# Gate and up projections by pairs of tiles: four of sixteen k blocks as two 2x2 block products of seven, and both tiles transposed together

## What is computed

```python
def _swiglu(x, w_gate, w_up, w_down):
    return (jax.nn.silu(x @ w_gate) * (x @ w_up)) @ w_down

x = _layer_norm(DEEPNORM_ALPHA * x + m, ln1_g, ln1_b)
x = _layer_norm(DEEPNORM_ALPHA * x + _swiglu(x, w_gate, w_up, w_down), ln2_g, ln2_b)
```

## Time and profile before

| | us |
|---|---|
| median of 3 runs | 943.72 (943.58 to 944.22) |
| the profiled execution, its own time | 944.1 |
| its span (first to last instruction) | 942.3 |
| PE busy in the span | 936.5 |
| DVE busy | 707.5 |
| ACT busy | 470.6 |
| POOL busy | 85.3 |

### The profile page before, as it was taken

The page is one execution under the profiler, slowest core; times in us unless marked ns, Lnnn a source line. Parts: engine busy times, 40 slices in busy tenths (PEclk is TensorE's granted clock), DMA queues, the critical chain, the costliest instruction groups (busy, mean ns, idle before and its releaser), DMA issues.

```text
span 942.3 us, 12166 instructions
## 1 busy us (share of the span) xinstructions
PE 936.5 (99%) x4466; PEld 786.0 (83%) x4466; DVE 707.5 (75%) x1146; ACT 470.6 (50%) x644; POOL 85.3 (9%) x78
## 2 busy tenths in 40 slices
PE   9999999999999999999999999999999999999997
PEld 8999988888888888888888888888888888888885
DVE  6778566588687776777777776776779987799777
ACT  5686764463444444444444444444445654465550
POOL 0105530000022020202020300000000000000000
PEclk9999999999999999999999999999999999999999
DMA  9844224593555655555555555555547666356632
GB/s 362 321 149 167 103 90 179 186 362 128 217 196 206 209 193 184 204 191 183 206 190 178 178 193 209 203 195 183 205 152 288 253 236 243 134 195 236 237 135 90
DMA packets 28102, 187.81 MB, mean 199 GB/s; under 512 B 3104, under 2 KB 3616, under 8 KB 6560
## 3 DMA queue, kind: packets, MB, share of 16 engines
q1 hardware_dynamic: 28032, 187.31, 54.5%
q0 software_dynamic: 32, 0.00, 0.0%
HBM read 183.11 MB, written 4.19 MB: 199 GB/s over the span
## 4 chain that ended last, share of the span: by engine, by line
PE 99%; DVE 0%; ACT 0%; DVEq 0%; issue 0%; ACTq 0%
PE acc L1535 58%; PE acc L1732 20%; PE acc L1473 5%; PE tp L1732 4%; PE acc L1394 4%; PE acc L1672 2%; PE acc L1507 1%; PE tp L1586 1%; PE tp L1521 1%; PE tp L1599 1%; PE tp L1383 0%; PE tp L1612 0%; PE tp L1611 0%; PE tp L1610 0%; PE tp L1628 0%; PE acc L1798 0%
## 5 line engine op out<-in xcount | busy, mean ns | idle before, releaser
L1535 PE MATMUL acc<-w_hi,act_t 128*128 128x512 f32 x1344 | 413.9, 389 | 0.0
L1038 DVE TENSOR_TENSOR w_lo<-raw,w_hi 128x1024 fp32r<-128x1024 f32 x191 | 236.3, 1251 | 124.8 <-ACT w_hi L753 123.9
L753 ACT ACTIVATE w_hi<-raw 128x1024 fp32r<-128x1024 f32 x184 | 194.8, 1061 | 246.3 <-PE acc L1535 244.3
L1535 PEld LDWEIGHTS acc<-w_hi,act_t 128*128 128x128 f32 x1344 | 252.4, 188 | 52.2
L1535 PE MATMUL acc<-w_lo,act_t 128*128 128x512 f32 x672 | 261.5, 389 | 0.0
L853 ACT ACTIVATE w_hi<-raw 128x512 fp32r<-128x512 f32 (+1 forms) x154 | 115.2, 782 | 100.1 <-PE acc L1732 85.9
L1732 PE MATMUL acc<-w_hi,hid_t 128*128 128x512 f32 x504 | 161.1, 389 | 0.0
L1217 DVE TENSOR_TENSOR w_lo<-raw,w_hi 128x512 fp32r<-128x512 f32 (+1 forms) x154 | 131.6, 880 | 35.9 <-ACT w_hi L853 35.6
L1535 PEld LDWEIGHTS acc<-w_lo,act_t 128*128 128x128 f32 x672 | 126.2, 188 | 26.3
L1732 PEld LDWEIGHTS acc<-w_hi,hid_t 128*128 128x128 f32 x504 | 94.6, 188 | 19.7
L1186 DVE STREAM_TRANSPOSE turned<-hid 32x128 f32<-32x128 f32 x352 | 106.6, 303 | 5.6
(11 more groups left out here) (214 smaller groups left out, 982.1 us busy)
## 6 DMA issues: line engine op xcount, KB each, us to landing
raw<-in_w_gu SPq DMA_DIRECT2D x88, 1024.0 KB, 4.8
raw<-in_w_down SPq DMA_DIRECT2D x44, 1024.0 KB, 5.0
raw<-in_w_out SPq DMA_DIRECT2D x16, 1024.0 KB, 4.8
raw<-in_x_w SPq DMA_DIRECT2D x14, 552.0 KB, 7.2
raw<-in_w_uq SPq DMA_DIRECT2D x4, 1024.0 KB, 7.7
raw<-in_w_ukv SPq DMA_DIRECT2D x4, 1024.0 KB, 6.0
ln_rows<-in_ln_rows SPq DMA_DIRECT2D x4, 1024.0 KB, 10.3
raw<-in_w_qidx SPq DMA_DIRECT2D x2, 1024.0 KB, 6.1
```

What stands on the lines that cost most here:

```text
L753: act.activation(w_hi[:, (2 * slot + half) % RING, 0:n], raw[:, slot, first:first + n], ACT.Copy).then_inc(hi_done, 1)
L1038: dve.tensor_tensor(w_lo[:, h, 0:n], raw[:, slot, first:first + n], w_hi[:, h, 0:n], ALU.subtract).then_inc(lo_done, 1)
L1535: last = pe.matmul(acc[:, bank0 + t, :], lhs[:, k, x, t * P:(t + 1) * P], part[:, w, n * GC:(n + 1) * GC], start=(start and x == 0 and par ...
```

## The change

Tiles 2 to 21 become ten pairs (p = 1 to 10; tile 2p is "first", 2p+1 is "second"). For four of the 16 k blocks the pair is one problem of two 2x2 blocks: (two halves of the tokens) x (two k blocks) times (two k blocks) x (two tiles), done twice for the two groups q of k blocks, and summed. The seven products are P1, P5, P6, P7, P2, P3, P4 in this order, each 2 groups x 3 = 6 matmuls. The left factors are blocks of the input or their sums `s_gate`, formed once by POOL. The right factors are blocks of the weights or their sums, which DVE forms in place in `raw` (`pair_sum`, four of 1024 columns for each pair). The other 12 k blocks are six plain steps for each tile. A step is still 1024 columns of `w_hi` and `w_lo`. The order of the steps is `FFN_STEPS`: the last three plain steps of the second tile of the pair before, seven products, six plain steps of the first tile, three of the second.

The products share banks. P1 goes to bank 1 of the second tile and stays there; P6 is added to it in place, then P7. After P1, after P6 and after P7 ACT copies that bank to another one (`seeded`): into the first tile's bank 0, negated into the second tile's bank 0, into the first tile's bank 1. There P2, P3 and P4 and the plain steps are added. P5 has a bank of its own, `tp[2]`; ACT copies it to `y_s` and DVE adds it to the second tile (`add_y`).

Transposes are done for both tiles of a pair at once: 16 instructions for a pair, each over 256 elements of a partition where it was 128, in four lots behind steps 2 to 5 of the next pair's first tile. `hid_hi` and `hid_lo` are one instruction for a pair. The first sum that POOL made is now made in place in `turned`, so `s_t` has three sums. Weights of a pair are loaded as 12 pieces of 512 KB and two of 1 MB; the first pair's two go to `quad_1`.

```diff
+def ffn_sequence():
+    steps = []
+    for p in range(1, PAIRS):
+        ends = [(p - 1, "second", n) for n in range(PLAIN - 3, PLAIN)] if p > 1 else [None] * 3
+        steps += ends + [(p, "product", n) for n in (P1, P5, P6, P7, P2, P3, P4)] + [(p, "first", 0)]
+        steps += [(p, "first", n) for n in range(1, PLAIN)] + [(p, "second", n) for n in range(PLAIN - 3)]
@@ SP
+            load_tile(0)
+            for q in range(2):
+                load_quad(1, q)
+            load_tile(1)
+            for n in range(PLAIN_SLOTS):
+                load_plain(1, n)
             sp.wait_ge(x1_done, TOK * CHUNKS)
             sp.dma_start(x1_rows, xn[:]).then_inc(x1_stored, 16)
@@ ACT
+            def hi_step(p, kind, n):
+                v = V_OF[p, kind, n]
+                if kind == "product":
+                    if n == P1:
+                        for q in range(2):
+                            act.wait_ge(quad_full[q], 16 * p)
+                    elif n in SUM_OF:
+                        act.wait_ge(pair_t_done, 4 * (p - 1) + SUM_OF[n] + 1)
+                    act.wait_ge(*used_step(v - RING))
+                    act.activation(by_quad(w_hi[:, v % RING, :]), quad(p, SOURCE[n]), ACT.Copy).then_inc(hi_done, 1)
...
+            def before_hi(v):
+                for p in range(1, PAIRS):
+                    first, second = banks_of(2 * p), banks_of(2 * p + 1)
+                    for n, dst, sign in ((P1, first[:, 0, :], 1.0), (P6, second[:, 0, :], -1.0),
+                                         (P7, first[:, 1, :], 1.0)):
+                        if v == V_OF[p, "product", n] + RING:
...
+                            act.wait_ge(*used_step(V_OF[p, "product", n]))
+                            act.activation(dst, second[:, 1, :], ACT.Copy, scale=sign).then_inc(seeded, 1)
...
+                if v - RING in FFN_ENDS:
+                    silu_step(2 + FFN_ENDS.index(v - RING))
@@ DVE
+            for p, kind, n in FFN_STEPS:
+                before_lo(V_OF[p, kind, n])
+                lo_step(p, kind, n)
+                if (kind, n) == ("product", P1):
+                    pair_sum(p, B11, B11, B12)
+                    pair_sum(p, B12, B12, B22)
+                if (kind, n) == ("product", P5):
+                    pair_sum(p, B11, B11, B22)
+                if (kind, n) == ("product", P2):
+                    pair_sum(p, B21, B11, B21)
+                if (kind, n) == ("first", 2):
+                    add_y(p)
+                if kind == "first" and n >= 2:
+                    turn_hid(p - 1, n - 2)
...
             for u in range(len(DOWN_UNITS)):
                 if u == 3:
-                    gate_up(TILES - 1, 1)
+                    gate_up(TILES - 1)
+                if u == 9:
+                    hid_lo(PAIRS - 1)
...
-                if u == 3:
-                    turn_hid(TILES - 1, (0, 1))
-                if u == 4:
-                    turn_hid(TILES - 1, (2, 3))
-                if u == 7:
-                    hid_lo(TILES - 1)
+                if 3 <= u < 7:
+                    turn_hid(PAIRS - 1, u - 3)
@@ PE
+            def pair_product(p, n):
+                first, second = banks_of(2 * p), banks_of(2 * p + 1)
+                out = {P1: second[:, 1, :], P5: tp[:, 2, :], P6: second[:, 1, :], P7: second[:, 1, :],
+                       P2: first[:, 0, :], P3: second[:, 0, :], P4: first[:, 1, :]}[n]
...
+                if n in (P6, P7, P4):
+                    pe.wait_ge(seeded, 3 * p - 2 + (P6, P7, P4).index(n))
+                pe.wait_ge(lo_done, v + 1)
+                for q in range(2):
+                    for x, part in ((0, w_hi), (0, w_lo), (1, w_hi)):
+                        last = pe.matmul(out, factor(q, Q_FACTOR[n], x), part[:, v % RING, q * GC:(q + 1) * GC],
...
```

More of the change, by code:

```diff
@@ L822, in ffn_tile @@
                     if h == 3:
-                        silu_step(i - 1, 1 - c)
+                        silu_step(0)
                     if h == 6:
[L825 to L837, removed]
+                        act.wait_ge(x1_stored, 16)
+                        act.wait_ge(g_step, 5)
+                        act.activation(s_gate[:, 0, :, :, :], g_sum[:], ACT.Copy).then_inc(g_hi, 1)
+            SOURCE = {P1: B11, P5: B11, P6: B11, P7: B12, P2: B21, P3: B22, P4: B21}
@@ L840, in down_hi_unit @@
+            tile_1()
+            for p, kind, n in FFN_STEPS:
+                before_hi(V_OF[p, kind, n])
+                hi_step(p, kind, n)
+                if (kind, n) == ("second", PLAIN - 4):
+                    hid_hi(p - 1)
+                if (kind, n) == ("product", P5) and 2 <= p < len(DOWN_QUADS) + 2:
+                    q = p - 2
+                    act.wait_ge(s_step, 4 * q + 4)
+                    act.activation(s_t[:, q, 0, :, :], s_sum[:], ACT.Copy).then_inc(s_hi, 1)
             def down_hi_unit(u):
@@ new lines, in pair_sum, with before_lo @@
+            def pair_sum(p, dst, x, y):
+                dve.tensor_tensor(quad(p, dst), quad(p, x), quad(p, y), ALU.add).then_inc(pair_t_done, 1)
+            def before_lo(v):
+                if v - RING in FFN_ENDS:
+                    gate_up(2 + FFN_ENDS.index(v - RING))
+                if v - RING == V_PAIRS - 1:
+                    gate_up(1)
+                for p in range(1, PAIRS):
+                    if v == V_OF[p, "second", PLAIN - 4] + 1:
+                        hid_lo(p - 1)
@@ new lines, in pair_plain @@
+            def pair_plain(p, tile, n):
+                out = banks_of(2 * p + (tile == "second"))
+                v, k0, end = V_OF[p, tile, n], PAIR_K + 2 * n, n == PLAIN - 1
+                if (tile, n) == ("first", 0):
+                    pe.wait_ge(seeded, 3 * p)
+                if (tile, n) == ("second", 0):
+                    pe.wait_ge(y_added, 2 * p)
+                pe.wait_ge(lo_done, v + 1)
+                for m in range(2):
+                    for t in range(TOK):
+                        for x, part in ((0, w_hi), (0, w_lo), (1, w_hi)):
+                            last = pe.matmul(out[:, t, :], act_t[:, k0 + m, x, t * P:(t + 1) * P],
+                                             part[:, v % RING, m * GC:(m + 1) * GC], start=False,
+                                             stop=(end and (m, x) == (1, 1)), skip_group_check=True)
+                last.then_inc(*((ffn_full, 1) if end else (pe_used, 1)))
@@ L1724, in _ @@
+            first_tile()
+            tile_1()
+            for p, kind, n in FFN_STEPS:
+                if kind == "product":
+                    pair_product(p, n)
+                else:
+                    pair_plain(p, kind, n)
             begun = {}
@@ L1828, in down_slot @@
         return down[list(tiles), :, :, pair, int(kind[1]) - 1].transpose(2, 0, 1, 3).reshape(P, -1)
+    gu = k_tiles(np.stack([gate, up], axis=2).reshape(D, 2 * FFN), 2 * FC)
+    later = gu[2:].reshape(PAIRS - 1, 2, P, KD, 2 * FC)
+    quads = later[:, :, :, 0:PAIR_K].reshape(PAIRS - 1, 2, P, 2, 2, 2 * FC).transpose(0, 2, 3, 1, 4, 5)
+    plain = later[:, :, :, PAIR_K:].transpose(0, 2, 1, 3, 4).reshape(PAIRS - 1, P, -1)
     arrays = {
```

325 lines of the change are left out of this document (231 added, 94 removed).

## The result

The median of the changed kernel is **952.21 us** (950.01 to 953.17, 4 runs), beside 943.97 us (943.58 to 944.51, 4 runs) for the kernel before: ratio 1.0084, interval 1.0069 to 1.0099. It is slower by 8.2 us; the forecast was 941.5 us, with a range from 939 to 948. The profiled execution took 951.89 us, its span is 950.1.

The account below looks back on a forecast made before the run. PE was taken as the bound, busy 99% of the span. -13.6 (matmuls) + 9.3 (gaps at P7) + 2.1 (start of down) = -2.2 us, for a median of 941.5 us, range 939 to 948.

Parts of the forecast that it names:

- Term 5, edges, at nothing: Tile 1: first pair's loads and store of x1 cost nothing; 1 or 2 us once if late; late-load chance 0.04.
- The lock between POOL and DVE: Third sum in seven pairs: DVE stretched by 0.17 us, not stopped; if held for 1.30, +7.7 us (949.2), chance 0.05.
- Term 1: Matmuls on PE: 186 instead of 192 for a pair, 60 fewer over ten pairs, -13.6 us.
- Term 2: Seven products: PE waits 0.93 us ahead of P7 for ACT's copy of P6, ten pairs, +9.3 us.
- Term 3: Turning in gate/up: transposes of 256 elements take 0.449 us, DVE's work fits, cost nothing.
- Term 4: Start of the down projection: 2.7 us more on DVE ahead of unit 9, PE waits +2.1 us over units 8 to 11.
- Copy 2 comes late: Rival, products: DVE/ACT chain x longer delays each P7 by x - 0.2; 945.5 us at x = 0.6; chance 0.17.
- DVE becomes the bound: Rival, transposes: at 0.628 us each they use up DVE's cover in the pairs and delay down; 955 us; chance 0.07.
- Milder gaps: Rival, P7 and start of down: copy 2 at 0.5, no 0.15 behind it, down term at nothing; 937 us; chance 0.17.

Follow-up runs that it names:

- e1: Changed kernel with the store of x1 placed ahead of the first pair's four plain loads on SP's queue: 945.59 us.
- e5: e3 with the last pair's four turning lots and its high and low parts spread over units 11 to 55 of the down projection: 940.97 us.
- e3: Changed kernel with both the store of x1 ahead of the plain loads and ACT's copy of `s_t` made earlier: 942.46 us.
- e2: Changed kernel with ACT's copy of `s_t`, and with it POOL's low part, moved four steps earlier: 946.74 us.
- e2b: Changed kernel with ACT's copy of `s_t` left in place and POOL's low part alone made later, behind the products: 946.72 us.
- e8: e1 with P2 ahead of P7, POOL's low part of `s_t` left on DVE's third sum: 938.86 us.

## Why the prediction was wrong

**The step that failed most: "Term 5, edges, at nothing".** It put the store's issue at 250, its landing at "perhaps 8" us, and so its end at 258, a microsecond inside ACT's cover; and it priced the loss of that cover at "1 or 2 us once". The issue was at 252.9, the landing took 10.2 us, the end was 263.1. The issue was late because DVE's four low parts of tile 1 took 8.36 us, 2.1 each on the mean, beside POOL's work on the input; I had not set the two against each other. The landing was longer than the 6.4 us of the earlier trace rows. In the changed kernel four loads were issued in the 5.4 us before it; in e1 six of 1 MB were issued between 14 and 4 us before it, and it took 10.3 us there as well. That loads still on their way are the cause fits both, but no run of the new order has the store without them. With a margin of 1 us on a sum of three estimates this needed a chance of its own, not 0.04. And the price was 4 us, not 1 or 2, with up to 3 us more for a clock that then falls: behind ACT's wait of 5.8 us stood POOL's low part of the input's sums, which then held DVE for 1.37 us on the path. The two failed steps met here.

**The second: "The lock between POOL and DVE".** I read the earlier trace rows as a hold of 0.17 us for each low part under a POOL instruction of 1.30, "stretched, not stopped", and gave the whole lock 0.05. The same rows say otherwise. POOL's instruction ends at 524.09 + 1.30 = 525.39, DVE's begins at 525.00, so they overlap by 0.39 us. The first of the two low parts takes 1.48 us, ending at 526.47, so 0.25 of the 2.70 - 2.36 = 0.34 is its loss; the other 0.08 is the second's, beside POOL's next instruction (525.34 to 526.62). In the changed kernel the overlap is 404.34 - 403.38 = 0.96 and the loss 0.82. Both times DVE's end is POOL's end, less 0.14, plus DVE's own 1.22, and so it is for the low part of 265.15 (266.65 - 0.14 + 1.22 = 267.73, for 267.74): it is stopped until POOL is nearly through. The Trainium skill had stated this ("SBUF — State Buffer", Who interferes with whom): the one that starts first keeps the shared ports for its whole instruction, and the other blocks. By that rule, the traces of before and after agree.
The size I had worked out for it, +7.7, was too large as well: the hold is not POOL's length but the overlap, 0.82 us, and 0.39 of it was slack (my chain from high P6 to copy 2 has 5.09 us, the trace has 405.46 to 410.26, 4.80, so copy 2 had 0.4 to spare, not 0.13). It cost 0.43 in seven pairs.

**What held.** Term 1: 60 matmuls fewer at the same distance. Term 2, in the pairs that POOL leaves alone: 43.12 - 42.16 = 0.96 us for each P7, 0.93 predicted, by the path named (0.67 idle, and the first matmuls start slower, 0.3). Term 3: 0.436 us for a transpose, 0.44 predicted, no wait of PE in the lots. Term 4: +2.4, predicted 2.1, and e5 removes 1.9 of it. The difference is a reading: the sum took the chain's 722.33 for the start of unit 11, whose first matmul is at 722.16, so the slack was 0.56 and not 0.7, and the sum should have been 2.3. Their sum was -2.2, and e3, which has neither of the two losses, measures -1.4 (942.46 against 943.83). The forecast came out on the wrong side because both errors are of one kind, something late for DVE or ACT, in a change whose own gain was only 2 us.

The parts, against the span's +7.8: -13.6 matmuls, +9.6 gaps, +3.0 POOL, +5.6 tile 1, +2.4 start of down, together +7.0. Of the other 0.8 us, 0.3 lie ahead of tile 1 (its first matmul is at 247.84, before at 247.53; in the eight other executions of changed kernels it lies between 246.8 and 247.9), 0.2 behind unit 11 (from there to the end 220.36 us, before 220.16), and 0.3 are not assigned.

**Of the rivals,** "Copy 2 comes late" is what happened in seven pairs, by another cause than the two it named. "DVE becomes the bound" and "Milder gaps" did not occur. What I should have seen as the larger point is that the gap at P7 was work missing on PE, not a price of the scheme: 9.6 of the 13.6 us gained were given back there, and the order of the products alone returned 8.0.

## What to carry to other kernels

When two instructions of DVE and POOL seem to disturb each other a little, compare the loss of each single instruction with the time by which the two overlap, not with the length of either; then look where the new order puts them on top of each other. When a store or a load is moved in a queue, work out its issue from the instructions that now stand ahead of it, each with its wait, and give a margin under 2 us a chance of its own. A dependency that goes from PE over ACT back to PE cost 0.96 us here each of ten times, with nothing else for PE between; an independent product put there returned 0.8 of it.

## What the runs showed of the hardware

A wait of 2.4 us on PE was followed by some 3.4 us at half the clock in two profiles (the changed kernel, means of 0.59 and 0.56 in two stretches of 2 us; e2, 0.61 and 0.53), and by none in a third (e2b); ten waits of 0.7 us each were followed by no fall in e3. A DVE operation of two inputs that began while a POOL instruction ran ended 1.08 us behind POOL's end (four cases: overlaps of 0.39, 0.96 and 1.50 us with losses of 0.25, 0.82 and 1.37, and 0.96 again in e8). Four low parts of 1.14 us each took 8.36 us beside POOL instructions of 1.60 to 2.41 us. A store of 2 MB landed in 6.4 us by itself, and in 7.9 to 10.3 in the changed kernels, with loads issued ahead of it.
